# State-space scan inputs: two full-precision products in two row groups, or three rounded products each in one

## The reference, cut to what matters

```python
def s5_scan(u, a_re, a_im, log_dt, b_re, b_im, c_re, c_im, d_skip):
    uf = u.astype(f32).reshape(bsz, seqlen, SSM_GROUPS, SSM_GROUP)
    ...
    bu_re = jnp.einsum('blgh,gph->blgp', uf, bbar_re)
    bu_im = jnp.einsum('blgh,gph->blgp', uf, bbar_im)
    ...
    _, _, x_re, x_im = lax.associative_scan(combine, (a_seq_re, a_seq_im, bu_re, bu_im), axis=1)
    y = (jnp.einsum('blgp,ghp->blgh', x_re, c_re.astype(f32))
         - jnp.einsum('blgp,ghp->blgh', x_im, c_im.astype(f32))
         + uf * d_skip.astype(f32))
```

## Time and profile before

| | |
|---|---|
| time, median of 3 runs | 2463.9 us (2462.94 to 2464.26) |
| the profiled execution | 2464.41 us |
| its span in the trace | 2462.6 us |
| PE busy | 2444.3 us, 99% of the span |
| PE weight loads busy | 1992.2 us, 81% |
| DVE busy | 1334.0 us, 54% |
| ACT busy | 940.7 us, 38% |
| POOL busy | 293.0 us, 12% |
| mean granted clock of PE | 0.999 |

### The profile page before, as it was taken

The page is one execution under the profiler, slowest core; times in us unless marked ns, Lnnn a source line. Parts: engine busy times, 40 slices in busy tenths (PEclk is TensorE's granted clock), DMA queues, the critical chain, the costliest instruction groups (busy, mean ns, idle before and its releaser), DMA issues.

```text
span 2462.6 us, 31484 instructions
## 1 busy us (share of the span) xinstructions
PE 2444.3 (99%) x12348; PEld 1992.2 (81%) x12348; DVE 1334.0 (54%) x1761; ACT 940.7 (38%) x1359; POOL 293.0 (12%) x237
## 2 busy tenths in 40 slices
PE   9999999999999999999999999999999999999998
PEld 7876988889876888888988888877778788888886
DVE  7774732434977563243543437768995386333322
ACT  4345532323445453232432235522335554322321
POOL 1231000001122100000111123400000121111101
PEclk9999999999999999999999999999999999999999
DMA  4312222223231222222222235643342143222222
GB/s 165 141 44 69 86 103 102 85 103 103 78 128 35 103 84 93 97 99 93 83 102 102 93 104 176 207 161 116 141 139 92 53 162 129 94 93 102 76 100 81
DMA packets 46253, 259.64 MB, mean 105 GB/s; under 512 B 5504, under 2 KB 6016, under 8 KB 23232
## 3 DMA queue, kind: packets, MB, share of 16 engines
q1 hardware_dynamic: 43712, 248.42, 28.9%
q0 software_dynamic: 640, 5.51, 0.6%
q10 hardware_dynamic: 1792, 4.20, 0.5%
HBM read 240.27 MB, written 16.78 MB: 104 GB/s over the span
## 4 chain that ended last, share of the span: by engine, by line
PE 92%; DVE 5%; ACT 2%; issue 1%; DMA 0%; SPq 0%; DVEq 0%; ACTq 0%
PE gemm L451 75%; DVE out_sb L1598 2%; PE gemm L733 1%; PE gemm L744 1%; PE gemm L735 1%; PE gemm L698 1%; PE gemm L699 1%; PE gemm L696 1%; DVE w_lo L401 1%; PE score L2126 1%; PE gemm L626 1%; ACT w_hi L393 1%; PE score L1124 1%; PE gemm L627 1%; PE gemm L635 1%
## 5 line engine op out<-in xcount | busy, mean ns | idle before, releaser
L401 DVE TENSOR_TENSOR w_lo<-w_raw,w_hi 128x2048 fp32r<-128x2048 f32 (+2 forms) x207 | 438.3, 2117 | 480.2 <-ACT w_hi L393 479.7
L451 PE MATMUL gemm<-h_hi,w_hi 128*128 128x512 f32 x1744 | 691.2, 396 | 1.2 <-DVE w_lo L401 0.7
L451 PE MATMUL gemm<-h_hi,w_lo 128*128 128x512 f32 x1744 | 679.9, 390 | 0.0
L451 PE MATMUL gemm<-h_lo,w_hi 128*128 128x512 f32 x1744 | 679.2, 389 | 0.0
L393 ACT ACTIVATE w_hi<-w_raw 128x2048 fp32r<-128x2048 f32 (+3 forms) x217 | 381.9, 1760 | 345.1 <-PE gemm L451 302.7
L451 PEld LDWEIGHTS gemm<-h_hi,w_hi 128*128 128x128 f32 x1744 | 327.8, 188 | 80.4 <-issue 7.8
L451 PEld LDWEIGHTS gemm<-h_hi,w_lo 128*128 128x128 f32 x1744 | 327.4, 188 | 69.4
L451 PEld LDWEIGHTS gemm<-h_lo,w_hi 128*128 128x128 f32 x1744 | 327.8, 188 | 65.8 <-issue 1.0
L451 PE MATMUL gemm<-f_hi,w_hi 128*128 128x512 f32 x448 | 174.3, 389 | 0.0
L451 PE MATMUL gemm<-f_lo,w_hi 128*128 128x512 f32 x448 | 174.3, 389 | 0.0
L451 PE MATMUL gemm<-f_hi,w_lo 128*128 128x512 f32 x448 | 174.3, 389 | 0.0
(11 more groups left out here) (462 smaller groups left out, 3844.8 us busy)
## 6 DMA issues: line engine op xcount, KB each, us to landing
w_raw<-in_w SPq DMA_DIRECT2D x171, 1024.0 KB, 4.8
w_raw<-in_w SPq DMA_DIRECT2D x16, 768.0 KB, 4.2
w_raw<-in_w SPq DMA_DIRECT2D x16, 640.0 KB, 3.8
w_raw<-in_w SPq DMA_DIRECT2D x18, 512.0 KB, 3.6
trig_kept<-made SPq DMA_DIRECT2D x16, 512.0 KB, 5.7
trig<-trig_kept SPq DMA_DIRECT2D x16, 512.0 KB, 6.2
bias_t<-in_att_bias SPq DMA_DIRECT2D x2, 1536.0 KB, 8.1
decay_t<-in_c_decay SPq DMA_DIRECT2D x2, 1536.0 KB, 8.1
```

The lines of the kernel that those rows point to most:

```text
L401: dve.tensor_tensor(flat(w_lo, b), flat(w_raw, b), flat(w_hi, b).bitcast(F32), ALU.subtract).then_inc(S["w_rest"], 1)
L451: mm = pe.matmul(dst, lhs, rhs, start=b.first and k == 0 and j == 0, stop=b.last and k == b.kt - 1 and j == 2)
```

## The change

`scan_in` makes six fp32r products in place of two f32 ones: for the real and for the imaginary part each, rounded B by rounded u, the rest of B by rounded u, and rounded B by the rest of u. All six use the row group `rows_of(s, 0)`. ACT makes the rounded operands (`u_hi`, four tiles, right after the evacuation of each `u` piece; `b_hi` in place of `b_turned`) and DVE the rests (`u_lo`, `b_lo`). `roll`, `u_roll` and its eight DMAs go, and POOL writes the imaginary table without the exchange, in two copies and not in four. The first two tiles of rounded u and of rests lie where `xq` will be, so the first evacuation of `xq` waits for step 7's products. The last rest of u is made in step 11, since it shares its place with the third.

```diff
-        MATS = 10
+        MATS = 8
...
                 if s % 4 == 0:
                     pe.wait_ge(S["bt_s"], a + 1)
-                    pe.wait_ge(S[f"rolled{a % 2}"], 32 * (a // 2 + 1))
+                    pe.wait_ge(S["u_lo_s"], a + 1)
                 if s:
                     pe.wait_ge(S["bu_read"], s)
-                for j, u in enumerate((u_sb[:, a, :], u_roll[:, a % 2, :])):
-                    r = rows_of(s, j)
-                    mm = pe.matmul(s_ps[j][:], b_turned[r, a % 2, P * j:P * j + P], u[r], start=True, stop=True)
+                r = rows_of(s, 0)
+                for j in range(2):
+                    c = slice(P * j, P * j + P)
+                    pe.matmul(s_ps[j][:], b_hi[r, a % 2, c], u_hi[a][r], start=True, stop=False)
+                    pe.matmul(s_ps[j][:], b_lo[r, a % 2, c], u_hi[a][r], start=False, stop=False)
+                    mm = pe.matmul(s_ps[j][:], b_hi[r, a % 2, c], u_lo[a][r], start=False, stop=True)
                 mm.then_inc(S["bu_ps"], 1)
...
-                for half in range(2):
-                    to, src = slice(2 - 2 * half, 4 - 2 * half), slice(2 * half, 2 * half + 2)
-                    pool.tensor_copy(b_all[r, 1, :, to, c], im[:, :, src, :]).then_inc(S["mats"], 1)
+                pool.tensor_copy(b_all[r, 1, :, :, c], im).then_inc(S["mats"], 1)
...
             for b in plan2[AT2["u"]:AT2["q"]]:
                 evacuate(b, lambda m: u_sb[:, 2 * (b.i - AT2["u"]) + m, :])
+                for a in range(2 * (b.i - AT2["u"]), 2 * (b.i - AT2["u"]) + 2):
+                    act.wait_ge(S["g_free"], plan2[AT2["u"]].t0 + a + 1)
+                    if a >= 2:
+                        act.wait_ge(S["mats"], MATS)
+                    act.activation(u_hi[a], u_sb[:, a, :], ACT.Copy).then_inc(S["u_hi_s"], 1)
                 round_block(act, b.n + 2)
 
             def copy_b(a):
                 act.wait_ge(S["turned_b"], a + 1)
                 if a >= 2:
                     act.wait_ge(S["bu_ps"], 4 * (a - 1))
-                act.activation(b_turned[:, a % 2, :], t_ps[:, 0:2 * P], ACT.Copy).then_inc(S["bt_s"], 1)
-
-            def roll(a):
-
-                act.wait_ge(S["g_free"], plan2[AT2["u"]].t0 + a + 1)
-                if a >= 2:
-                    act.wait_ge(S["bu_ps"], 4 * (a - 1))
-                for r in range(2):
-                    to, src = slice(HD * (1 - r), HD * (1 - r) + HD), slice(HD * r, HD * r + HD)
-                    act.dma_start(u_roll[to, a % 2, :], u_sb[src, a, :]).then_inc(S[f"rolled{a % 2}"], 16)
-
-            act.wait_ge(S["mats"], MATS)
-            for a in range(2):
-                roll(a)
+                act.activation(b_hi[:, a % 2, :], t_ps[:, 0:2 * P], ACT.Copy).then_inc(S["b_hi_s"], 1)
+
             copy_b(0)
...
+                        if b.i == AT2["xq"] and m == 0:
+                            act.wait_ge(S["bu_ps"], 8)
...
-                    if s in (4, 8):
-                        roll(s // 4 + 1)
...
+            def rest_u(a):
+                dve.wait_ge(S["u_hi_s"], a + 1)
+                if a == 3:
+                    dve.wait_ge(S["bu_ps"], 4 * a)
+                dve.tensor_tensor(u_lo[a], u_sb[:, a, :], u_hi[a].bitcast(F32),
+                                  ALU.subtract).then_inc(S["u_lo_s"], 1)
+
+            def rest_b(a):
+                dve.wait_ge(S["b_hi_s"], a + 1)
+                if a >= 2:
+                    dve.wait_ge(S["bu_ps"], 4 * (a - 1))
+                dve.tensor_tensor(b_lo[:, a % 2, :], t_ps[:, 0:2 * P], b_hi[:, a % 2, :].bitcast(F32),
+                                  ALU.subtract).then_inc(S["bt_s"], 1)
+
             for b in plan2[AT2["u"]:AT2["q"]]:
+                for a in range(2 * (b.i - AT2["u"]), 2 * (b.i - AT2["u"]) + 2):
+                    if a < 3:
+                        rest_u(a)
                 rest_block(dve, b.n + 2)
+            rest_b(0)
...
                 dve.tensor_tensor(tmp2[:, 1, :], br, sin, ALU.mult).then_inc(S["bu_read"], 1)
+                if s % 4 == 1 and s + 3 < STILES:
+                    rest_b(s // 4 + 1)
+                if s == 11:
+                    rest_u(3)
```

More of the change, by code:

```diff
@@ L1824, in build @@
         c_all = at("c_all", [P, 2, STILES, SSM_G * 2], F32, FZ + 72)
-        u_roll = at("u_roll", [P, 2, SEQ], F32, FZ + 62)
-        b_turned = at("b_turned", [P, 2, 2 * P], F32, FZ + 76)
+        u_hi_near = at("u_hi_near", [P, 2, SEQ], F32R, FZ + 16)
+        u_lo_near = at("u_lo_near", [P, 2, SEQ], F32R, FZ + 20)
+        u_hi_far = at("u_hi_far", [P, 2, SEQ], F32R, FZ + 62)
+        u_lo_far = at("u_lo_far", [P, SEQ], F32R, FZ + 66)
+        u_hi = [u_hi_near[:, 0, :], u_hi_near[:, 1, :], u_hi_far[:, 0, :], u_hi_far[:, 1, :]]
+        u_lo = [u_lo_near[:, 0, :], u_lo_near[:, 1, :], u_lo_far[:], u_lo_far[:]]
+        b_hi = at("b_hi", [P, 2, 2 * P], F32R, FZ + 76)
+        b_lo = at("b_lo", [P, 2, 2 * P], F32R, FZ + 78)
         time_t = at("time_t", [P, SEQ], F32, 64)
@@ L1893, in build @@
                   "trig_s", "trig_moved0", "trig_moved1", "trig_moved2", "rotated", "summed", "scanned", "z_sin_s", "z_cos_s", "real_s", "x_kept_s", "x_back", "coef_a", "coef_r",
-                  "coef_t", "bbar_s", "turned_b", "bt_s", "rolled0", "rolled1", "real_read", "half_read", "values_turned", "values_kept", "bu_ps", "bu_read", "state_s", "y_ps", "y_read", "y_s", "gelu_s",
+                  "coef_t", "bbar_s", "turned_b", "b_hi_s", "bt_s", "u_hi_s", "u_lo_s", "real_read", "half_read", "values_turned", "values_kept", "bu_ps", "bu_read", "state_s", "y_ps", "y_read", "y_s", "gelu_s",
                   "t5_in", "s2_ps", "s2_bias", "s2_max", "s2_exp", "s2_prob", "s2_turn_ps", "s2_turn", "s2_mix", "s2_out",
```

## The result

The changed kernel takes 2472.38 us (median of 7 runs, 2471.9 to 2472.62), the kernel before, run beside it, 2464.2 us (2462.94 to 2465.03). The ratio is 1.0033 with a 95% interval of 1.0024 to 1.0043: 8.2 us slower, where 7.9 was forecast (2471.8 us on the median). The profiled execution took 2471.95 us, 1.9 above its span of 2470.1.

What follows compares the result with a forecast made beforehand. PE, busy 99% of the span, was taken as the bound: 16 x 0.51 - 0.2 = +7.9 us on the 2463.9 us median gave 2471.8 us. Its own range was 2470.8 to 2473, for 8 in 10 2468.5 to 2476.5.

Steps and rivals of the forecast that it cites:

- PE bounds the stretch, and its time is paid in full: PE is busy 99% of the span; scan_in lies on the chain 16 times, each step adding 0.51 us.
- The pair ran side by side: In scan_in before, two f32 products overlap in two row groups: 1.05 us, against 1.71 one after the other.
- Six products at 0.227: In the new scan_in, each 32-row fp32r product costs 0.227 us like 128 rows: 1.36, or 1.56 with the shape change.
- The 0.20 stays with fp32r: In each scan_in, 0.20 us belongs to the change of tile shape; rival that fp32r pays less: +4.7 to +7, chance 0.16.
- Bare weight loads: Rival: loads of the six scan_in products are not overlapped, +17 to +24 us, 2481 to 2488, chance 0.08.
- Preparation is free: New copies on ACT and rests on DVE, some 4.4 us on DVE, cost PE 0, up to 0.5 us once.
- The slack at step 0: DVE's rest of B is ready 0.15 us before PE wants step 0.
- The wait at step 15 goes: PE's 0.21 us wait for DVE before step 15's output disappears, since PE arrives 1.5 us later: -0.2 us.
- Cheap products and hidden time: Rival: scan_in's products cost under 0.175 us each (2461 at 0.15), or added time is hidden, 0.7 at most; chance 0.03.

Runs made afterwards that it cites:

- Run 1: Kernel before with both f32 products of scan_in in one row group, without the second copy of u and the exchanged imaginary table: 2477.6 us, 1.0054.
- run 3: Changed kernel with its six rounded products in two row groups, real and imaginary part issued by turns: 2461.78 us, 0.9991.
- run 4: Changed kernel without the product of B's rest by rounded u, so two products for each part: 2465.17 us, 1.0004.
- run 5: Changed kernel with its six products over all 128 rows and not the step's 32: 2468.13 us, 1.0016.
- Run 2: Changed kernel with all its new ACT, DVE and POOL work, but one f32 product for each part in two row groups: 2464.39 us, 1.0000.
- run 6: Changed kernel with one fp32r product of 96 rows for each part, without the copies this needs: 2459.1 us, 0.998.
- run 7: Changed kernel with three terms stacked by POOL's DMAs, one 96-row product for each part, ACT and DVE reordered: 2461.8 us, 0.9989.
- run 8: As run 7, with DVE's last w_lo of the projections moved behind the last state: 2459.94 us, 0.9983 against the kernel before.

## Why the prediction was right

- **PE bounds the stretch, and its time is paid in full: right.** +0.53 us a step in the timeline, +8.34 in the stretch, +8.2 in the medians. Runs 1, 3 and 4 move the time by what the steps' records say, to within the waits that they add. The 0.3 us between forecast and measurement are 16 times the 0.02 by which the step was longer than 1.56.
- **The pair ran side by side: right, and shown.** Run 1 costs +0.86 a step (1.91 for 1.05), run 3 gives 0.90 for the same products that cost 1.58 in one group.
- **Six products at 0.227: right.** 0.232 in the trace, 0.225 to 0.24 by run 4. This was the term that no row showed. "From below, the same as 128 rows" is what holds; run 5 shows it the other way round.
- **The 0.20 stays with fp32r: right.** 1.58 is 6 x 0.227 and 0.22: 0.11 for the bare first load, 0.09 at the exit to 32 columns, and 0.02 that the products took above 0.227. Run 5 takes the change of rows away and gets 0.22 a step back, which is another sum: 0.09 ahead of the first product, 0.11 for its load and 0.02 on the others. The 0.09 at the exit stays.
- **Bare weight loads: a wrong rival.** Five of six loads of 0.18 us lie under a product of their own row group, and the step is 1.58, not 2.55. By the Trainium skill ("TensorE: Matmul & The Clock Gate", on the mechanism of packing small products) a load overlaps a product in flight only in another row group. The trace decides against that sentence for these tiles. The same section also lets a load run ahead when it goes to a background weight buffer; the trace fits that, but no run shows that this is how it happens.
- **Preparation is free: right.** Run 2 is at 1.0000. The slack at step 0 was 0.2 us, forecast 0.15.
- **The wait at step 15 goes: right, 0.21.** Its other side is seen in runs 3 and 6: where PE gets faster, the wait grows, by 0.5 and 1.3 us.
- **Cheap products and hidden time: wrong**, as expected: no product was under 0.22. The break-even price of 0.175 us (1.05 / 6) was also set too high, since it leaves out the 0.20 of the shape change that the sum itself keeps; with it, it is 0.85 / 6 = 0.14. That only makes this rival weaker.

## What to carry to other kernels

Before exact f32 products are exchanged for rounded ones, count them as they run and not as they stand: two f32 products side by side cost 1.05 us here, six rounded ones in one row group 1.58, the same six in two groups 0.90, and two stacked ones of 96 rows 0.56. Products of 32, 96 and 128 rows cost the same here, so it pays to put short operands below one another, and an idle queue can carry them there. And a gain on PE is only as large as the slack of the engine that feeds it: of the 9.7 us that the stacked products save in PE's records, run 6 lost 4.0 to waits for DVE, and some 1.6 more to the lower clock that PE was granted behind two of these waits.

## What was new of the hardware

That fp32r products of 32 rows run side by side in two row groups like f32 ones (six in 0.90 us) was seen here for the first time. Also new was that 96 small DMAs from POOL's queue, 4.7 MB in the 16 steps, landed in 1.7 to 7.0 us each while DVE was busy nine tenths of the time, and that PE never waited for one of them; the tables of angles, however, landed in 6.8 us in the median where it had been 5.7.

A short wait can cost PE its clock. In runs 6, 7 and 8 the granted clock fell from 2.4 to 1.2 GHz (1.00 to 0.50) near 1712 us, for less than 4 us: in run 6 behind waits of 1.21 and 1.06 us with only the mixed products between them, in run 8 behind 2.20 and 1.06, in run 7 right behind a wait of 1.85. Waits of 1.53 and 1.51 us at step 15 of runs 6 and 7 left it at 1.00, and in the traces of the two kernels and of runs 1 to 5 it is 1.00 from 10 to 2450 us. Which of these waits it takes, and why, isn't shown.
